# Hybrid S5 and DeltaNet encoder layer with a hierarchical MoE: the router computed tile by tile inside the out projection, and every expert given the block of its own number

## The reference

```python
x = x + jnp.concatenate([y_s5, y_dn], axis=-1) @ w_out[i]      # 1024 x 1024
h = _rmsnorm(x, norm_ffn[i]).reshape(bsz * seq, d)
...
g_logits = h @ w_rg + b_rg                                     # 4 groups
g_prob = softmax(g_logits); _, g_sel = lax.top_k(g_logits, 1)
e_logits = (logits of the 8 experts of group g_sel)
top_val, top_idx = lax.top_k(e_logits, 2)
gate = softmax(top_val) * p_group
expert_idx = g_sel * 8 + top_idx                               # 2 of 32 experts a token
...
# the 2048 assignments are sorted by expert and filled into blocks of 128 rows
hid = silu(xb @ w_gate[e]) * (xb @ w_up[e]); y = hid @ w_down[e]
x = x + sum over the token's two rows of gate * y ; x = _rmsnorm(x, norm_final)
```

## Time and profile before

| | |
|---|---|
| median of 3 runs | 1445.21 us (1443.62 to 1445.22) |
| profiled execution: time | 1439.3 us |
| profiled execution: span from first to last instruction | 1437.6 us |
| PE / DVE / ACT / POOL busy | 91% / 74% / 60% / 30% |
| mean granted TensorE clock | 0.955 |
| gate and up matmuls (each of the three lines) | x528, that is 16 for each of 33 blocks |

### The profile page before, as it was taken

How to read it: one execution, slowest core, us unless ns; L and a number is a source line. 1 busy time by engine, 2 the same in 40 slices (tenths; PEclk the granted TensorE clock), 3 DMA queues, 4 the chain that set the end, 5 groups by cost and what they waited for, 6 DMA issues and landing times. The chain is left out here.

```text
span 1437.6 us, 24617 instructions
## 1 busy us (share of the span) xinstructions
PE 1312.8 (91%) x8394; PEld 1107.2 (77%) x8394; DVE 1059.4 (74%) x1330; ACT 861.5 (60%) x1162; POOL 432.8 (30%) x473
## 2 busy tenths in 40 slices
PE   4999999978898979999964899999999999999994
PEld 3999778867787878668854688888888888888871
DVE  5895797775777758542137788888888888888847
ACT  7473445565555564552122577777777777777742
POOL 6020099018656737312201111111111111111130
PEclk9999999978999989999975999999999999999997
DMA  9174987411234139801124899999999999999865
GB/s 268 47 227 145 284 243 226 112 41 51 47 87 133 26 121 344 303 16 44 45 107 151 325 391 417 412 411 411 404 416 411 411 413 411 410 409 412 364 234 217
DMA packets 154680, 357.49 MB, mean 249 GB/s; under 512 B 43983, under 2 KB 100587, under 8 KB 127467
## 3 DMA queue, kind: packets, MB, share of 16 engines
q1 hardware_dynamic: 131755, 297.04, 55.3%
q0 software_dynamic: 14976, 40.43, 8.3%
q10 hardware_dynamic: 7872, 19.01, 3.4%
HBM read 287.64 MB, written 68.78 MB: 248 GB/s over the span
## 5 line engine op out<-in xcount | busy, mean ns | idle before, releaser
L2839 PE MATMUL gate_up_mm<-w_hi,gathered_T_hi 128*128 128x512 f32 x528 | 213.2, 404 | 7.8 <-DVE gathered_T_lo L3022 7.8
L2841 PE MATMUL gate_up_mm<-w_hi,gathered_T_lo 128*128 128x512 f32 x528 | 208.2, 394 | 0.0
L2840 PE MATMUL gate_up_mm<-w_lo,gathered_T_hi 128*128 128x512 f32 x528 | 207.8, 394 | 0.0
L3017 DVE TENSOR_TENSOR w_lo<-w_down,w_hi 128x2048 fp32r<-128x2048 f32 x66 | 148.5, 2289 | 54.6 <-ACT w_hi L2945 54.6
L2790 POOL COPY gather_idx<-slot_token 128x1 int32 (+1 forms) x34 | 25.9, 763 | 476.3 <-PE x_turned L2829 449.4
L3017 DVE TENSOR_TENSOR w_lo<-w_gate,w_hi 128x2048 fp32r<-128x2048 f32 x66 | 150.8, 2289 | 19.2 <-ACT w_hi L2945 18.1
L2945 ACT ACTIVATE w_hi<-w_gate 128x2048 fp32r<-128x2048 f32 x66 | 126.9, 1923 | 52.4 <-PE gate_up_mm L2841 31.5
L2945 ACT ACTIVATE w_hi<-w_up 128x2048 fp32r<-128x2048 f32 x66 | 126.7, 1923 | 49.9 <-PE down_mm L2876 49.9
L3017 DVE TENSOR_TENSOR w_lo<-w_up,w_hi 128x2048 fp32r<-128x2048 f32 x66 | 150.7, 2287 | 4.1 <-ACT w_hi L2945 0.5
L2945 ACT ACTIVATE w_hi<-w_down 128x2048 fp32r<-128x2048 f32 x66 | 125.1, 1918 | 40.7 <-issue 20.8
L2839 PEld LDWEIGHTS gate_up_mm<-w_hi,gathered_T_hi 128*128 128x128 f32 x528 | 100.8, 191 | 34.2 <-issue 11.9
(11 more groups left out here) (506 smaller groups left out, 3093.5 us busy)
## 6 DMA issues: line engine op xcount, KB each, us to landing
w_down<-in_expert_w_down SPq DMA_DIRECT2D x66, 1024.0 KB, 7.1
w_gate<-in_expert_w_gate SPq DMA_DIRECT2D x64, 1024.0 KB, 7.5
w_up<-in_expert_w_up SPq DMA_DIRECT2D x64, 1024.0 KB, 8.3
expert_rows_dram<-ones SPq DMA_DIRECT2D x32, 512.0 KB, 6.8
expert_rows_dram<-expert_out ACTq DMA_DIRECT2D x32, 512.0 KB, 8.6
x<-s_rows_dram SPq DMA_DIRECT2D x9, 1184.0 KB, 7.9
s_rows<-s_rows_dram SPq DMA_DIRECT2D x7, 1184.0 KB, 7.5
w_raw<-in_w_in SPq DMA_DIRECT2D x12, 512.0 KB, 5.3
```

What stands on the lines that cost most here:

```text
L2839: pe.matmul(dst, xT_hi[:, k, :], hi[:, at, cols], start=k == 0, stop=False)
L2840: pe.matmul(dst, xT_hi[:, k, :], lo[:, at, cols], start=False, stop=False)
L2841: mm = pe.matmul(dst, xT_lo[:, k, :], hi[:, at, cols], start=False, stop=k == KT - 1)
L3017: dve.tensor_tensor(lo[:, at, :], flat(j), hi[:, at, :].bitcast(F32), ALU.subtract).then_inc(S["piece_lo"], 1)
```

## The change

The block `router` is gone, and its work is in three places.

In the out projection, `pick(t)` (17 DVE steps on one tile's 36 logits: group, two experts, their one-hot rows, and their sum `both`) and `place(t)` (10 or 11 DVE steps and two one-hot tiles: the token's rank inside its expert, from PE's `rank(t)`, and its row in a table of 128 slots x 256 columns) run per tile. DVE's order is place(t - 2), x1 of t, pick(t - 1), the norm of t. PE's order is pieces 0 to 7 of `project(t)`, rank(t - 2), table(t - 3), route(t - 1), pieces 8 to 11, logit(t - 1), pieces 12 to 15. The table's columns 0 to 31 are the first 128 rows of each expert, and the others hold rows beyond 128 by expert and level; no column depends on another expert's count. POOL makes the constants once.

Blocks 0 to 31 are now the experts 0 to 31, whatever their counts; blocks from 32 on are the further ones. Which column and which expert they are is found in `experts`, in DVE's `block_table()` with a few PE transposes and matmuls, ahead of `rest(0, 0)`. The first gather takes column 0 at once. The number of blocks is loaded by each engine only ahead of the loop. POOL loads each block's column number too. The weights of expert 0 are loaded at the start of `experts`, in four pieces. The gates and the slot numbers (`dest`) are computed in `places()`, which grows.

```diff
@@ s5_and_projection, tensor
-            for t in range(TT + 2):
-                if t < TT:
-                    project(t)
...
-                if t >= 2:
-                    logit(t - 2)
-                if 1 <= t <= TT:
-                    route(t - 1)
+            for t in range(TT):
+                project(t, 0, 8)
+                if t >= 2:
+                    rank(t - 2)
+                if t >= 3:
+                    table(t - 3)
+                if t >= 1:
+                    route(t - 1)
+                project(t, 8, 12)
+                if t >= 1:
+                    logit(t - 1)
+                project(t, 12, 16)
...
+            rank(TT - 2)
+            route(TT - 1)
+            table(TT - 3)
+            logit(TT - 1)
+            table(TT - 2)
+            rank(TT - 1)
+            table(TT - 1)
@@ s5_and_projection, vector
             for t in range(TT):
+                if t >= 2:
+                    place(t - 2)
                 dve.wait_ge(Q["mm"], t + 1)
                 dve.tensor_tensor(x1[:, t, :], x1[:, t, :], mm_ps[:, t % 2].rearrange("p a n -> p (a n)"), ALU.add
                                   ).then_inc(Q["x1"], 1)
+                if t == 1:
+                    dve.wait_ge(Q["made"], ROUTE_MADE)
+                if t >= 1:
+                    pick(t - 1)
                 dve.wait_ge(Q["sq"], t + 1)
...
+            place(TT - 2)
+            pick(TT - 1)
+            place(TT - 1)
+            dve.wait_ge(Q["table"], TT)
+            dve.tensor_copy(c["pair"][:].bitcast(I32), table_ps).then_inc(Q["slots"], 1)
+            dve.wait_ge(Q["slots"], 1)
@@ new: pick(t), the part that repeats for the two experts k
+                for k in range(2):
+                    top, place = kept["top"][:, k, t:t + 1], kept["down_e"][:, k, t:t + 1]
+                    picks.done()
+                    picks(dve.tensor_reduce(top, em, AX.X, ALU.max))
+                    picks.done()
+                    picks(dve.scalar_tensor_tensor(out=peak, in0=em, scalar=top, in1=r["down"][:], op0=ALU.is_ge,
+                                                   op1=ALU.mult))
+                    picks.done()
+                    picks(dve.tensor_reduce(place, peak, AX.X, ALU.max))
+                    picks.done()
+                    picks(dve.tensor_scalar(r["one"][:, n, k], r["down"][:], place, None, ALU.is_equal))
@@ new on PE
+            def rank(t):
+                pe.wait_ge(Q["both"], t + 1)
+                pe.wait_ge(Q["summed"], t + 1)
+                pe.matmul(pos_ps, r["strict"][:], r["both"][:, t % 2], start=True, stop=False)
+                mm = pe.matmul(pos_ps, c["ones"][:], r["sum"][:], start=False, stop=True)
...
+            def table(t):
+                pe.wait_ge(Q["placed"], 2 * (t + 1))
+                for k in range(2):
+                    mm = pe.matmul(table_ps, r["hit"][:, t % 2, k, :], r["cell"][:, t % 2, k, :],
+                                   start=t == 0 and k == 0, stop=t == TT - 1 and k == 1)
@@ experts, sync
-            sp.wait_ge(early, 32)
-            first = expert(0)
...
+            for j in range(4):
+                load(j, 0)
+            sp.wait_ge(S["tables"], 3)
+            count = sp.value_load(rt["count"][0:1, 0:1], min_val=NEXP, max_val=MAXB)
@@ experts, gpsimd
             gather(0, 0, 1)
...
+            pool.memset(whole[:], 1.0).then_inc(S["made"], 1)
+            pool.iota(bound[:], [[P, LEVELS]], base=0, channel_multiplier=0, **loose).then_inc(S["made"], 1)
+            pool.iota(reach[:, 0:NEXP], [[1, NEXP]], base=1, channel_multiplier=0, **loose).then_inc(S["made"], 1)
...
@@ experts, vector
+            block_table()
             for j in range(3):
                 rest(0, j, j + 1)
             rows_rest(0)
             rest(0, 3, 4)
             places()
@@ new: block_table(), its two waits on PE
+                dve.wait_ge(S["made"], 5)
...
+                dve.wait_ge(S["reach_turned"], 1)
...
+                dve.wait_ge(S["reach_turned"], 2)
```

More of the change, by code:

```diff
@@ L2047, in s5_and_projection @@
     S = {n: core.sem("s5m_" + n) for n in names}
[L2048 removed]
+    names = ("w_ld x_ld w_hi y_hi w_lo y_lo par mm x1 sq ms rt rs h turned hT lg store0 store1 made both ranked summed "
+             "placed table pick_step place_step slots").split()
     Q = {n: core.sem("op_" + n) for n in names}
@@ L2171, in turn_gated, with project @@
                 mm.then_inc(S["gated_turned"], 1)
-            def project(t):
-                if t < 2:
+            def project(t, first, end):
+                if first == 0 and t < 2:
                     pe.wait_ge(S["gate"], t + 3)
-                else:
+                elif first == 0:
                     pe.wait_ge(Q["x1"], t - 1)
-                for n, (k, half) in enumerate(PIECES):
+                for n in range(first, end):
+                    k, half = PIECES[n]
                     if n % 8 == 0:
@@ L2649, in experts, with route_buffers @@
-def experts(nc, core, c, a, rt, h_dram, y_dram, wg, wu, early, x1, out):
-    KD = DE // P
+        "group": core.sb("kept_group", [P, TT, NGRP], side="right"),
+        "top": core.sb("kept_top", [P, 2, TT], side="right"),
+        "down_e": core.sb("kept_down_e", [P, 2, TT], side="right"),
+        "level": core.sb("kept_level", [P, 2, TT], side="right"),
+        "slot": core.sb("kept_slot", [P, 2, TT], side="right"),
+        "count": core.sb("kept_count", [P, NEXP], side="right"),
+    }
+def route_buffers(core):
+    return {
+        "iota": core.sb("r_iota", [P, P]),
+        "token": core.sb("r_token", [P, TT]),
+        "down": core.sb("r_down", [P, NEXP]),
+        "bound": core.sb("r_bound", [P, LEVELS + 1]),
+        "strict": core.sb("r_strict", [P, P]),
+        "logit": core.sb("r_logit", [P, NGRP + NEXP]),
+        "best": core.sb("r_best", [P, 2]),
+        "one_g": core.sb("r_one_group", [P, NGRP]),
+        "masked": core.sb("r_masked", [P, NEXP]),
+        "peak": core.sb("r_peak", [P, NEXP]),
+        "one": core.sb("r_one", [P, 2, 2, NEXP]),
+        "both": core.sb("r_both", [P, 2, NEXP]),
+        "sum": core.sb("r_sum", [P, NEXP]),
+        "prod": core.sb("r_prod", [P, 2, NEXP]),
+        "rank": core.sb("r_rank", [P, 2]),
+        "over": core.sb("r_over", [P, 2, LEVELS + 1]),
+        "at": core.sb("r_at", [P, 2, LEVELS]),
+        "cell": core.sb("r_cell", [P, 2, 2, TABLE], F32R),
+        "hit": core.sb("r_hit", [P, 2, 2, P], F32R),
+    }
@@ new lines, in experts @@
+def experts(nc, core, c, a, kept, h_dram, y_dram, x1, out):
+    KD = DE // P
+    NB = MAXB + 2
+    wg, wu = core.sb("w_gate", [P, KT, DE]), core.sb("w_up", [P, KT, DE])
+    rt = {"slot_tok": c["pair"][:].bitcast(I32), "block": core.sb("block_expert", [P, NB], I32),
+          "column": core.sb("block_column", [P, NB], I32), "count": core.sb("block_count", [P, 1], I32),
+          "gate": core.sb("gate", [P, 2, TT])}
+    whole = core.sb("ex_ones", [P, TABLE - NEXP])
+    more = core.sb("ex_more", [P, NEXP, LEVELS - 1])
+    reach = core.sb("ex_reach", [P, TABLE])
+    starts = core.sb("ex_starts", [P, 2, NEXP])
+    bound = core.sb("ex_bound", [P, LEVELS])
+    primary = core.sb("ex_primary", [P, NB])
+    ends = core.sb("ex_ends", [P, 3])
+    past = core.sb("ex_past", [P, 3, NB])
+    found = core.sb("ex_found", [P, 2, NB])
+    one_e = core.sb("ex_one", [P, 2 * TT, NEXP])
+    small_cols = core.sb("ex_cols", [P, 6, 2 * TT])
```

409 lines of the change are left out of this document (209 added, 200 removed).

## The result

The kernel after runs in 1450.75 us (median of 20 runs, 1444.78 to 1460.46), the kernel before, on the same chip, in 1446.44 us (20 runs). The ratio is 1.0038, 95% interval [1.0025, 1.0052], so the change costs 3.6 to 7.5 us.

The account below looks back on a forecast made before the run. PE bounds the full block loop, a chain of small DVE steps the router. 15.3 - 17.3 + 7.3 = +5.3 on a profiled 1439.3 gives 1444.6; with 5.9 carried over to the median, 1450.5 us, 8-in-10 range 1442.5 to 1456.5.

Parts of the forecast that it names:

- Term 1: Out projection: the x1 of the last tile (X) moves by +15.3 us, as h waits for pick.
- Term 2: From the last tile's x1 (X) to the end of routing (D): 22.7 us instead of 40.0, a gain of 17.3.
- Term 3: From the end of routing (D) to the first gate matmul (M): 19.4 us instead of 12.11, +7.3.
- the weights' arm: Ahead of the first gate matmul, beside block_table() and rests: weight loads, fourth split and rows_out, done at 17.1 to 18.1 us.
- Shortening one alone would give at most 0.3: Ahead of the first gate matmul: block_table() with rests and weight loads with splits are nearly equally long; cutting one gives 0.3 us.
- places() at no cost: Behind the first gate matmul: places() grows to 22 steps, 10.4 us, but stays hidden with 0.6 us to spare.
- Had it no cover it would cost some 5: Start of block 1: the grown places() would cost some 5 us if nothing hid it.
- The price of a step: Small dependent DVE steps: 0.22 us each, 147 on the path, so 0.01 us a step is 1.5 us.
- Free waits: Rival, chance 0.20: the new DVE steps cost only 0.19 us each; +0.9, 1446.1 us.
- overlapping steps: Rival, chance 0.15: small DVE steps cost 0.15 us and the projection stall is gone; -5.0, 1440.2 us.
- Cold first block: Rival, chance 0.09: weights land later than 15.1 or PE stays at 1.2 GHz through block 0; +12.2, 1457.4 us.

Follow-up runs that it names:

- norm_first: Changed kernel with VectorE's norm of a tile ahead of pick(t - 1), and TensorE's rank after piece 11, logit and table after piece 15; ratio 1.0004 to before.
- table_plus8: Changed kernel with 8 more dependent 49-column VectorE steps at the end of block_table(), result unchanged; ratio 1.0047 to before.
- block0_order: Changed kernel with first rows' high part after the second weight split (ScalarE), low part after rest(0, 1) (VectorE); ratio 1.0017 to before.
- tail_order: norm_first with the last tile reordered: TensorE does transposes of h(7) and logit(7) before rank(6), VectorE pick(7) before place(6); ratio 0.9949 to before.
- before_pair: Kernel before with the two triangles of ones made halves of one tile, only addresses changed; ratio 1.0004 to before.
- picks_late: tail_order and block0_order together, with the 16 one-hot tiles ending places() made after the fourth rest of block 1; ratio 0.995 to before.
- pick_plus8: Changed kernel with 8 more dependent 32-wide VectorE steps in every pick(t), multiplying a scratch tile by 1; ratio 1.0161 to before.

## Why the prediction was right, point by point

The forecast was 1450.5 us, +5.3 on before; measured were 1450.75 and a difference of 3.6 to 7.5. The closeness to 0.3 us is in part luck: the forecast started from a median of three runs that lies 1.2 under that of the 20, and the terms below are all somewhat larger than predicted. The steps, against the trace:

- **Term 1, predicted +15.3, is +15.8.** The tile went from 13.75 to 15.45, predicted 15.5; h comes 6.9 behind x1, as worked out. The wait ahead of the transposes, called "some 1", is 0.70 in five of the six tiles and 1.02 in the first of them. The six tiles cost 10.2 (predicted 10.7), and the work that moved ahead of the last x1 4.6, as counted. The first interval, where a late h was said to cost nothing, took 1.0 more than its share of that work (15.73 against 11.94, of which 2.75 are one route and one logit): PE waited 0.86 for h(0). No pick had run, but the norm weights came late, and h itself took 1.72 instead of 1.28 beside a split on GpSimd (last section). Timeline of after:

```profile
651.55 1.72 DVE L2448 SCALAR_TENSOR_TENSOR h_row<-x,op_rs,after_sum 128x1024 f32<-128x1024 f32 x1 [1.06 <-DMA after_sum<-in_norm_ffn]
```

norm_first shows the mechanism: with h ahead of pick the wait is gone, and rank and table cost 0.75 a tile in the open.
- **Term 2, predicted 22.7, is 23.1.** pick(7) starts at X + 13.3 (predicted 13.1) and rank(7) with its crossing takes 2.0 (1.9). pick took 3.9, not 3.75. The remark that one tile's pick costs nearly what eight tiles' did is wrong: in the router block the same part, 21 steps for eight tiles at once, took 7.9 us, from 746.84 to 754.72, so one tile costs half of it. Timeline of before:

```profile
746.84 0.19 DVE L2568 TENSOR_REDUCE r_cols<-logits 128x8 f32<-128x32 f32 x1 [1.71 <-POOL r_iota L2518]
...
754.10 0.62 DVE L2595 TENSOR_TENSOR r_both<-r_one 128x256 f32<-128x256 f32 x1
```

- **Term 3, predicted 19.4, is 19.8.** block_table() ended 0.5 earlier than worked out (10.5), and the last weights landed later: their split began at D + 15.7, 0.6 behind the later bound of 15.1. So the weights' arm was the longer. table_plus8 confirms it: 1.8 us more on the other arm cost 0.3.
- **"Shortening one alone would give at most 0.3" held, the reading of it did not.** I took the order of the work in the two arms as given. Both end in pieces that the first matmul doesn't need, and block0_order took 3.25 us off with no work removed.
- **places() at no cost held**, with 1.6 to spare instead of 0.6. "Had it no cover it would cost some 5" is unproved: in block0_order, where the cover shrank, the rest behind it came 1.3 late and the first gate matmul of block 1 0.7.
- **The price of a step.** 16 steps of pick(7) take 3.74 from 767.84 to 771.58, 0.234 each; the added ones cost 0.21 (a scaling of 32 columns) to 0.235. *Free waits* (0.19) and *overlapping steps* (0.15) both fall. The Trainium skill (VectorE: DVE Perf Modes, section The DRAIN you can't avoid) has it that the semaphore costs nothing extra, measured on 8 copies that take 13.88 us together; for these small steps the traces disagree: a dependent one starts 0.02 to 0.04 behind the end of the one before, while two that need nothing of each other start closer than one is long (r_both at 713.08, 0.19 long, op_ms at 713.19).
- **Cold first block** did not come: 0.77 in both. The blocks are 33 in both (x528).

The sum over the stages of one execution of each kernel is +7.7, the prediction's terms +5.3, and the medians give +4.3. Terms 1 to 3 measured are +15.8, -16.9 and +7.7, together +6.6; the remaining +1.2 lies behind M, where the same stretch varies by 2.7 us between kernels (602.9 to 605.6), perhaps in part with when the clock rises: 2.9 us behind M in tail_order (602.9), some 5.5 in after and before_pair (605.6 and 605.1), but 6 in picks_late (604.7). I can't assign it to the change.

What the change was worth was thus not decided by its idea but by three places in the order: pick ahead of the norm (5.6 us up to D, with PE's order changed too), the order of the last tile (5.3 once the norm is first), and the splits ahead of the rows (3.3 at M; that it reaches the end is not shown). With the first two turned round the same change is 0.5% faster than before instead of 0.4% slower.

## What to carry to other kernels

Where work is moved under another engine's cover, price the cover at the point where it is put, not over the stage: DVE had 9.4 us idle in a tile, and yet 3.9 us of new steps made the tile 0.94 longer (15.45 against 14.51 in norm_first) where they stood ahead of the one result that PE waits for. Give each engine its work in the order in which others need it, and look at the last turn of a pipelined loop by itself, because there the cover of the next tile is missing. A chain of small dependent steps pays per step (0.21 to 0.235 us here), so splitting one pass over 8 tiles (7.9 us here) into 8 passes of 3.9 costs four times as much, and only pays under cover. And where a longer wait makes PE stand still, its granted clock can fall too, which cost some 1.4 us in each of three tiles of pick_plus8.

## What the runs showed of the hardware

**Operations of VectorE and of GpSimd with two inputs each held each other up.** In the tile of after shown above r_sum, 32 columns, takes 1.13 us beside GpSimd's split of y, against 0.18 to 0.19 in the last tile, where no split runs; it ends at 716.27, where GpSimd's operation ends (716.23). In norm_first it is h_row that pays, 2.41 instead of 1.28. The Trainium skill (SBUF — State Buffer, section Who interferes with whom) states that a VectorE instruction with two SBUF inputs contends with a GpSimd one that reads SBUF, and that the other blocks for its whole length; the trace agrees, the two ends lie within 0.04 us. In norm_first PE comes to the transposes later than h in any case, so it was hidden; in the first tile of after it lengthened a wait that showed.

**The end varies by 8 us between profiled executions.** From the last rows to the end it is 47.7 to 55.7. In the nine longer ones VectorE waits 3.4 to 7.4 us at one instruction of the final sum, which adds gathered rows; of after:

```profile
1421.10 1.28 DVE L3221 SCALAR_TENSOR_TENSOR x<-w_gate,gate_before_last,x_turned 128x1024 f32<-128x1024 f32 x1 [6.34 <-remote]
```

before and picks_late, with 48.1 and 47.7, have no such wait. Five of the nine traces name "remote" as the releaser, the others a PE instruction or none, so that a gather landed late is the likely cause, not a shown one. There is one profiled execution of each kernel; that the kernel doesn't decide it is seen in before and before_pair, which differ in addresses alone and have 48.1 and 54.8. It is why single executions could not be compared by their time here.
